# A three-block network in one kernel: block 1 normed ahead of its modulation, low halves on DVE, an unrolled conv FFN, and the bias store in sixteen transfers

## What is computed

```python
# block 1: both inputs are normed, scaled and shifted; then one dense product, retention and conv, 16 experts
sh1, sc1, g1, sh2, sc2, g2 = _modulation(c, w_ada, b_ada)          # silu(c) @ w_ada + b_ada
hc = _rms_norm(ctx, pre_mix_g) * (1.0 + csc1) + csh1               # context tokens
hx = _rms_norm(x,   pre_mix_g) * (1.0 + sc1)  + sh1                # the tokens themselves
... = split(hc @ w_in);  ... = split(hx @ w_in)
x = x + g1 * _rms_norm(mix_x, post_mix_g)
x = x + g2 * _rms_norm(_expert_choice_ffn(hx2, ...), post_ffn_g)
# block 2, second half
x = x + rmsnorm(merged @ w_out, mix_post_norm)
h = rmsnorm(x, ffn_pre_norm)
up = causal_dwconv(h @ w_ffn_up, ffn_conv_w, ffn_conv_b)           # 6144 channels, 3 taps
f_gate, f_val = split(up, 2)
x = x + rmsnorm((gelu(f_gate) * f_val) @ w_ffn_down, ffn_post_norm)
# block 3, attention with a relative bias: bias = rel_bias[t5_bucket(dist)], dist = query - key
```

## Time and profile before

| | |
|---|---|
| median of 3 runs | 2014.65 us (2014.63 to 2015.08) |
| the profiled execution's own time | 2014.23 us |
| its span, first to last instruction | 2012.4 us |
| mean granted clock of TensorE | 0.879 of full |
| PE / DVE / ACT / POOL busy | 1537.4 / 715.4 / 593.5 / 96.3 us |

### The profile page before, as it was taken

The page is one execution under the profiler, slowest core; times in us unless marked ns, Lnnn a source line. Parts: engine busy times, 40 slices in busy tenths (PEclk is TensorE's granted clock), DMA queues, the critical chain, the costliest instruction groups (busy, mean ns, idle before and its releaser), DMA issues.

```text
span 2012.4 us, 25017 instructions
## 1 busy us (share of the span) xinstructions
PE 1537.4 (76%) x10341; PEld 1036.4 (51%) x10341; DVE 715.4 (36%) x1136; ACT 593.5 (29%) x1009; POOL 96.3 (5%) x44
## 2 busy tenths in 40 slices
PE   4999886565666666566556569999879999898897
PEld 2787731111111111111111139989869888797897
DVE  3347320000000000000000028767667885558564
ACT  4443420000000000000000025765644553455453
POOL 1264300000000000000000000000000000000000
PEclk8999887888887878877788889999989998899899
DMA  9366559999999999999999983344554443443230
GB/s 402 135 251 243 240 242 427 429 429 428 429 429 428 429 428 429 429 429 428 428 429 428 429 350 143 134 147 148 161 150 164 174 155 138 157 150 133 85 126 22
DMA packets 48439, 570.10 MB, mean 283 GB/s; under 512 B 4592, under 2 KB 10736, under 8 KB 11888
## 3 DMA queue, kind: packets, MB, share of 16 engines
q1 hardware_dynamic: 40992, 556.81, 67.4%
q10 hardware_dynamic: 7376, 12.29, 2.5%
HBM read 564.89 MB, written 4.19 MB: 283 GB/s over the span
## 4 chain that ended last, share of the span: by engine, by line
PE 44%; DMA 39%; DVE 11%; ACT 3%; issue 2%; DVEq 1%; ACTq 1%; POOL 0%; SPq 0%
PE bank L1488 44%; DMA ring<-in_w_down 13%; DMA ring<-in_w_gate 12%; DMA ring<-in_w_up 12%; DVE ring_rounded L2078 2%; ACT work L1796 1%; DVE work L899 1%; DMA ring<-in_w_ada 1%; DVE rstd L2024 1%; ACT weights_high_rounded L1796 1%; DVE h_normed L2028 1%; DVE work L2028 1%; ACTq L660 1%; DVE work L895 0%; POOL ring_rounded L1473 0%
## 5 line engine op out<-in xcount | busy, mean ns | idle before, releaser
L1488 PE MATMUL bank<-ring,work 128*32 128x512 f32 x3008 | 481.2, 772 | 315.2 <-DMA ring<-in_w_up 126.4
L1796 ACT ACTIVATE work<-bank 128x256 f32<-128x256 f32 (+4 forms) x291 | 128.9, 453 | 1136.2 <-PE bank L1488 812.0
L1488 PEld LDWEIGHTS bank<-ring,work 128*32 128x32 f32 x3008 | 92.8, 125 | 671.3 <-DMA ring<-in_w_up 208.1
L2078 DVE TENSOR_TENSOR ring_rounded<-ring,weights_high_rounded 128x1024 fp32r<-128x1024 f32 x208 | 250.3, 1221 | 117.5 <-ACT weights_high_rounded L1796 117.4
L1796 ACT ACTIVATE weights_high_rounded<-ring 128x1024 fp32r<-128x1024 f32 x244 | 255.7, 1052 | 22.0 <-PE bank L1488 21.9
L2248 DVE TENSOR_TENSOR work<-work,bank 128x512 f32<-128x512 f32 x16 | 16.5, 1030 | 594.4 <-PE bank L1488 594.4
L1488 PE MATMUL bank<-h_high_rounded,weights_high_rounded 128*128 128x256 f32 x1296 | 202.1, 296 | 19.0 <-ACT h_high_rounded L1796 17.7
L1488 PEld LDWEIGHTS bank<-h_high_rounded,weights_high_rounded 128*128 128x128 f32 x1296 | 172.7, 194 | 36.6 <-issue 23.6
L1488 PE MATMUL bank<-h_high_rounded,ring_rounded 128*128 128x256 f32 x1296 | 181.1, 283 | 12.5 <-DVE ring_rounded L2078 12.0
L1488 PE MATMUL bank<-h_normed_rounded,weights_high_rounded 128*128 128x256 f32 x1296 | 181.3, 284 | 0.0
L1488 PEld LDWEIGHTS bank<-h_high_rounded,ring_rounded 128*128 128x128 f32 x1296 | 164.5, 193 | 15.7 <-DVE ring_rounded L2078 14.4
(11 more groups left out here) (225 smaller groups left out, 1168.2 us busy)
## 6 DMA issues: line engine op xcount, KB each, us to landing
ring<-in_w_down SPq DMA_DIRECT2D x64, 2048.0 KB, 16.3
ring<-in_w_gate SPq DMA_DIRECT2D x63, 2048.0 KB, 16.4
ring<-in_w_up SPq DMA_DIRECT2D x61, 2048.0 KB, 16.3
ring<-in_dense SPq DMA_DIRECT2D x60, 2048.0 KB, 8.0
ring<-in_w_ada SPq DMA_DIRECT2D x12, 2048.0 KB, 12.7
work<-in_w_up SPq DMA_DIRECT2D x3, 1024.0 KB, 13.3
bias_diagonals<-work ACTq DMA_DIRECT2D x2, 1532.0 KB
ring<-in_dense SPq DMA_DIRECT2D x2, 1024.0 KB, 18.8
```

The source lines that it names most:

```text
L1488: return nc.tensor.matmul(o, lhsT, rhs, start=start, stop=stop)
L1796: return nc.scalar.activation(o, i, f, **kw)
L2078: v.tensor_tensor(as_r(w), w, w_high[:, buffer, :], ALU.subtract).then_inc(s.w_low, 1)
```

## The change

Six edits, all in one diff.

1. **Start of block 1.** The sums of squares come ahead of ada products 1 to 3 on PE. DVE norms ctx and x (`CTXN`, `XN`) ahead of the modulation; when this is there, ACT (scale and bias) and DVE (`shifted_split`) each work out scaled and shifted tiles. The 655 KB of early constants are no longer part of the first constants' load but come after the second root. `first_jobs` takes the first four jobs tile by tile.
2. **Block 1's weight lows** (36) move from POOL to DVE, as `lows1` between its other operations. A 128x1024 reciprocal is two of 128x512 with a low between.
3. **Experts.** The last one is written out and ends the accumulation itself; the eight closing matmuls are gone.
4. **Bias store.** ACT's two DMAs become sixteen, one for each head and kind, each from one partition. SP issues them, behind rounds 1 to 5 of `dense2` (blocks 0 to 19) and ahead of block 20.
5. **FFN.** Unrolled. ACT applies one tap and the bias as it takes a unit out of PSUM; DVE adds the two shifted taps straight from PSUM; PE may reuse a bank when `conv_step` says that they are done. Gelu, product and splits of a pair follow at once.
6. **The wait for the store**, ahead of DVE's FFN before, is ACT's at unit 40 of 48.

```diff
 # SP
-            with sp.Fori(0, D2_BLOCKS // RING) as r:
+            def dense2_round(r):
                 for b in range(RING):
                     sp.wait_ge(s.ring_used, r * RING + (D2_BLOCK0 + b - RING + 1))
...
+            rounds_before = (L_SSM + 4) // (RING * UNITS) + 1
+            with sp.Fori(0, rounds_before) as r:
+                dense2_round(r)
+            sp.wait_ge(s.toep_sb, 3)
+            for kind in range(2):
+                for h in range(AH):
+                    sp.dma_start(d["toep"][kind * AH + h:kind * AH + h + 1],
+                                 spread(TW[h:h + 1, kind, :], 1, P)).then_inc(s.toep_stored, 16)
+            with sp.Fori(rounds_before, D2_BLOCKS // RING) as r:
+                dense2_round(r)
 # ACT, SSM units
                 if n == 3:
+                    fn(TW[0:AH, :, TOEP:TPITCH], ones[0:AH, 0:2].unsqueeze(2), ACT.Copy).then_inc(s.toep_sb, 1)
...
-                    act.wait_ge(s.toep_sb, 2)
-                    for kind in range(2):
-                        act.dma_start(d["toep"][kind * AH:(kind + 1) * AH, :, 0:TOEP],
-                                      spread(TW[0:AH, kind, 0:TOEP], 1, P)).then_inc(s.toep_stored, 16)
 # PE, FFN up
-            tensor_loop2(pe, dense_unit, L_UP, 3, normed, IN_AT["up"][0])
+            for u in range(2 * FT):
+                if u >= 4:
+
+                    pe.wait_ge(s.conv_step, taps_through(u - 4))
+                unit2(L_UP + u, normed, None if u else "up")
+            pe.wait_ge(s.conv_step, taps_through(2 * FT - 1))
 # ACT, FFN up
+            for u in range(2 * FT):
+                unit_done(d2_block(L_UP + u), block_ends(L_UP + u))
+                if u == 40:
+
+                    act.wait_ge(s.toep_stored, 32 * AH)
+                fn(ffn_conved(u), B[(PU2 + L_UP + u) % 4][:, 0:SEQ], ACT.Identity, scale=ffn_weight(u, 2),
+                   bias=par("ffn_conv_b", u, u + 1)).then_inc(s.dense_sb, 1)
+                weight_high(D1_UNITS + L_UP + u + AHEAD2)
 # DVE, FFN up (the loops with conv_pair go)
+            for k in range(FT):
+                for u in (2 * k, 2 * k + 1):
+                    tap(u, 1)
+                    weight_low(L_UP + u + AHEAD2)
+                    tap(u, 2)
+                    if u % 2 == 0 and k:
+                        split_low(FV[:, k - 1, :], UP[:, 2 * (k - 1), :])
+                dve.wait_ge(s.ffn_gelu, k + 1)
+                dve.wait_ge(s.conv_step, taps_through(2 * k + 1))
+                v.tensor_tensor(FV[:, k, :], FV[:, k, :], UP[:, 2 * k, :], ALU.mult).then_inc(s.act_full, 1)
 # experts, PE
-            for q in range(4):
-                last = mm(B[4 + q][:], ZERO[0:1, 0:P], ZERO[0:1, :], False, True)
-            last.then_inc(s.acc_done, 1)
+            expert(EXPERTS - 1, final=True)
 # block 1, DVE
-            norm_invert(0)
-            norm_invert(1)
+            for i, dst, src in ((0, CTXN, CTXR), (1, XN, X)):
+                norm_invert(i)
+                for half in (slice(0, 4), slice(4, KT)):
+                    v.tensor_tensor(dst[:, half, :], src[:, half, :], spread(RS[:, i, :], 1, 4),
+                                    ALU.mult).then_inc(s.first_normed, 1)
+            lows1(0, 1)
             modulation(0)
...
-            norm_shifted(0, HC, CTXR, A1[:, 1, :], MOD[:, 0:8, 1], CTXR)
-            norm_shifted(1, H, X, A1[:, 0, :], MOD[:, 0:8, 0], HH)
+            shifted_split(1, HC, CTXN, CTXR)
+            lows1(1, UNITS)
+            shifted_split(0, H, XN, HH)
```

More of the change, by code:

```diff
@@ L371, in tensor_dense2 @@
                        last).then_inc(s.ring_used if block_ends(unit) else s.dense_mm, 1)
[L373 to L381, removed]
         def conv_unit(u):
@@ L387, in conv_unit, with taps_through, ffn_weight, ffn_conved @@
             return dst, par(name + "_w", 4 * n, 4 * n + 4), par(name + "_b", n, n + 1)
+        def taps_through(u):
+            return 2 * u + 2
+        def ffn_weight(u, tap):
+            return par("ffn_conv_w", 3 * u + tap, 3 * u + tap + 1)
+        def ffn_conved(u):
+            return tiles(u - 1, 1) if u % 2 else tiles(48 + u // 2, 1)
         def tensor_block2(pe, mm, dense_unit, column_sum, column_sums):
@@ L504, in tensor_block2, with scalar_block2 @@
             column_sum(8, KT - 1)
[L506 to L527, removed]
+        def scalar_block2(act, fn, link, square, squares_of_x, root_table, root, unit_done, weight_high, split_high):
             def copy2(unit, dst, tile=None):
@@ L675, in scalar_block2 @@
                 split_high(HH[:, k, :], H[:, k, :])
[L677 to L693, removed]
+            for u in range(2 * FT):
[5 more added lines that the diff above has]
+                weight_high(D1_UNITS + L_UP + u + AHEAD2)
+                k = u // 2
+                if u % 2:
+                    act.wait_ge(s.conv_step, taps_through(u - 1))
                     fn(FV[:, k, :], FV[:, k, :], ACT.Gelu_apprx_tanh).then_inc(s.ffn_gelu, 1)
-                if k >= 18:
-                    split_high(UP[:, 2 * (k - 2), :], FV[:, k - 2, :])
+                elif k:
+                    split_high(UP[:, 2 * (k - 1), :], FV[:, k - 1, :])
+            split_high(UP[:, 2 * (FT - 1), :], FV[:, FT - 1, :])
             for n in range(KT):
@@ L1470, in _ @@
         def _(pool):
-            def low(block_no, sub, buffer):
-                w = unit_weights(block_no, sub)
-                nc.gpsimd.tensor_tensor(as_r(w), w, w_high[:, buffer, :], ALU.subtract).then_inc(s.w_low, 1)
-            for unit in range(D1_UNITS):
-                pool.wait_ge(s.w_high, unit + 1)
-                low(d1_block(unit), unit % UNITS, unit % HIGHS)
             for n in range(4):
@@ L1491, in arrived, with dense_unit @@
                 pe.wait_ge(ring_loaded[block_no % RING], uses(block_no))
-            def dense_unit(block_no, sub, bank, high, low, counts, base=None, first=True, last=True, turn=None):
+            def dense_unit(block_no, sub, bank, high, low, counts, base=None, first=True, last=True):
                 buffer = w_high[:, (counts - 1) % HIGHS, :]
-                if turn is not None:
-                    counts = turn + counts
                 parts = [("hh", buffer, high), ("lh", None, high), ("hl", buffer, low)]
@@ L1533, in column_sum @@
                 pe.wait_ge(s.norm_squared, KT * i + k + 1)
-                if i and k == 0:
+                if i > 1 and k == 0:
                     pe.wait_ge(s.norm_root, i)
-                last = mm(B[bank][:, 0:SEQ], ones[:], SQ[:, k, :], k == 0, k == KT - 1)
+                last = mm(B[bank][:, 0:SEQ], ones[:], (HH_plain if i == 1 else SQ)[:, k, :], k == 0, k == KT - 1)
                 if k == KT - 1:
@@ L1739, in expert @@
                                           k == 0, k == KT - 1)
-                        if not (isinstance(e, int) and 4 * half + b in EXTRA):
+                        if not (first and 4 * half + b in EXTRA):
                             last.then_inc(s.ring_used, 1)
@@ L2082, in weights_low, with lows1 @@
                     weight_low(unit)
+            def lows1(first, end):
+                for unit in range(first, end):
+                    dve.wait_ge(s.w_high, unit + 1)
+                    w = unit_weights(d1_block(unit), unit % UNITS)
+                    v.tensor_tensor(as_r(w), w, w_high[:, unit % HIGHS, :], ALU.subtract).then_inc(s.w_low, 1)
             def modulation(r):
@@ L2110, in _ @@
             last.then_inc(s.ramp_ready, 1)
-            dve.wait_ge(s.consts_in, 16)
+            lows1(4, 8)
+            dve.wait_ge(s.start_in, 32)
             dve.wait_ge(s.dense_sb, 2)
```

220 lines of the change are left out of this document (115 added, 105 removed).

## The result

The changed kernel takes 2043.2 us (median of 4 runs, 2039.67 to 2043.93) against 2014.87 (2014.63 to 2017.04) for the kernel before: 1.0135 times the time, 95% interval 1.0117 to 1.0152, 28.3 us slower. Its profiled execution took 2042.85 us (span 2041.1), 28.6 more than that of before.

What follows compares the result with a forecast made beforehand. PE bounds it wherever fed, DMA the experts. From 2014.2 us, block 1 -9.5, experts' end -3.6, FFN -20.4 and store +68.6 sum to +35.1: 2049.3 us; forecast's own range 2033 to 2066, 8 in 10 1969 to 2062.

Steps and rivals of the forecast that it cites:

- block 1's start and mix: Block 1: start gains 10.2 us, fewer POOL waits 0.7, two lows standing behind other work cost 1.4; net -9.5.
- experts' end: End of the experts: eight matmuls between the last product and ACT go away, -3.6 us.
- first up matmul, in times of before: FFN start: a 114 us store ahead of block 20 on SP's queue delays it to 1574.2 from 1505.62, +68.6 us.
- FFN: FFN's up product: PE stays the bound at conv-stage pace, one wait of about 4 us is left, -20.4 us.
- the overlap between groups: Store: reading ahead where one group of four partitions ends saves at most 24 us of 126; the middle, 12, was taken.
- The reading that decided: Old store: neither engines nor HBM limit it, but reading few partitions, about 25 GB/s per group of four.
- landing + 1.05 + 9.6: Ahead of the FFN: the first up matmul comes no sooner than block 20's landing plus these microseconds.
- The 9.3 us of ACT's hold: Bias store: freeing ACT of its 10.81 us issue would gain 9.3 us, but the slow store on SP swallows it.
- the account of DVE's room: FFN: a pair costs DVE 5.2 us against PE's 5.55, leaving 0.35 us to spare.
- rival (c): FFN: with a fast store DVE becomes the bound, giving back 13 us, and 4 in block 1; 1988 us, chance 0.05.
- Rival (a): Store: engines limit, so sixteen make it fast, 28 us, and all gains stand, -42.8; 1971 us, chance 0.22.
- Rival (b): Store: both groups of four partitions are read at once, 63 us at 50 GB/s; 1998 us, chance 0.12.

Runs made afterwards that it cites:

- e9: The kernel before with the three edits of block 1 alone (start, lows on DVE, last expert): 1997.44 us against 2012.67, ratio 0.9918.
- e4: The kernel before with the store edit alone (sixteen transfers on SP): 2078.31 us, 62.8 above before, ratio 1.031.
- e5: The kernel before with the FFN edit alone, ACT waiting for the old store at unit 40: 1994.26 us, 20.9 below before, ratio 0.989.
- e1: The changed kernel with the store's heads in the order 0,4,1,5,2,6,3,7 instead of 0 to 7: 2000.22 us, ratio 0.9925 to before.
- e2: The changed kernel with the store as two transfers of eight partitions each, at the same place in SP's queue: 1997.23 us, ratio 0.9908 to before.
- e3: The changed kernel with the bias table made in all 128 partitions and stored by two transfers on SP's queue: 1969.33 us, ratio 0.9766 to before.
- e6: The kernel before with the table made in all 128 partitions, its two store transfers still on ACT's queue: 2006.56 us, 8.6 below before, ratio 0.9951.
- e8: e3 with the third tap of the FFN's conv back on DVE, from PSUM, ACT only copying: 1974.13 us, 4.8 above e3.
- e7: e3 with block 1's 36 weight lows given back to POOL: 1975.15 us, 5.8 above e3.

## Why the prediction was right

The point was 2049.3, the result 2043.2 (profiled 2042.85): slower, as forecast, by the mechanism forecast, and inside the forecast's own range (2033 to 2066). By its terms, in the traces of before and after:

| term | forecast | measured | from |
|---|---|---|---|
| block 1's start and mix | -9.5 | -8.9 | squares after the experts 12.6 sooner, less 3.6 |
| experts' end | -3.6 | -3.6 | the closing matmuls' 3.64 are gone |
| first up matmul, in times of before | +68.6 | +62.3 | 1555.29 + 12.6 - 1505.62 |
| FFN | -20.4 | -20.8 | start of block 3's long run +28.84, less 49.67 |
| sum | +35.1 | +28.8 | 28.84 before rounding |

The measured column is one pair of traces, and each entry is good to about 2 us: by the means of ten traces (under e9) the first line is -10.7. Its entries add up by the way they are taken, so the sum is no test of its own; the test is that e4, e5 and e9 measure the parts one by one (+62.8, -20.9, -15.2).

**The store is the term that was mis-sized**, by 6.3 us, and that it is no more is in part luck: three errors in its working partly cancel. The rate of one group of four partitions is 27.4 GB/s (7.18 us a transfer), not 25, so 115 us of reading instead of 126. The store's packets pass from 1433.5 to about 1535.3, where GB/s rises from 25 or so to over 300 in the DMA view: 102 us, so the overlap between groups was 13 us, near the 12 taken. That is 12 us less than the 114 forecast, at the low end of its 102 to 126. But the store began 1.5 us later than forecast, and block 20 then took 9.5 us to land, not 4.9. SP had put three loads of the ring into the queue by 1537.6, and 3.69 MB passed in those 9.5 us, of which block 20 is 2.1: it had to share the engines, and the forecast took it to be alone:

```profile
1525.57 12.05 SPq L1408 DMA_DIRECT2D ring<-in_dense  x3
```

A packet took 0.69 us, not the 0.9 that was named as a sign; still three times the 0.22 of before.

The Trainium skill ("SBUF — State Buffer", "Door 1: The DMA port swizzle") gives 27.6 GB/s for partitions 0 to 3; the trace agrees, with 27.4. Its figure was nearer to the measured rate than the 25 that the sum used.

**The reading that decided**, from the last microsecond of the old store (fewer engines, shorter packets, nearly the same rate), is borne out by e1 (order alone, 43 us), e2 and e3. That all sixteen engines shared one transfer, as the change made them, was true and no help.

**The stage behind it**, landing + 1.05 + 9.6, held: 1544.84 to 1555.29 is 10.45. The 9.3 us of ACT's hold were swallowed in the change, as forecast, and show as 8.6 in e6, where nothing else holds the stage's end.

**FFN**: PE stays the bound, one wait of 3.25 where about 4 was said. But the account of DVE's room was too tight. It added the mean durations of DVE's operations. In e8 the six groups' busy times add up to 87.1 us in a window of 80 us: operations in a row overlap at their ends, so a sum of durations overstates what they take. In the change DVE is busy 17.23 of 20 us, which leaves about 0.8 us a pair in place of the 0.35 that was worked out, so rival (c) was less likely than the 0.05 it had.

**Block 1**: the fifth job came at 59.80, forecast 60.3. The terms for the waits in the middle (+0.7, -1.4) and for the end of the mix (nothing) are known only in their sum with the start.

Rival (a), 1971, is what e3 makes of the same edits with a fast store: 1969.3. Rival (b), 1998, is what e1 and e2 make with both groups read at once: 2000.2 and 1997.2. Their prices were right; their condition wasn't met.

## What to carry to other kernels

Count the partitions that are read at a time, not the engines that a transfer spreads over: here one partition after another out of a group of four gave 27 GB/s, both groups together about 50, all 128 partitions about 370. Nothing between 8 and 128 was tried. A table that is to be written many times is better made in all partitions first (here one small copy and a wider stationary operand). A queue that carries weights takes only stores that are fast. When an edit bundle gets slower, don't give up the bundle: here one part cost 63 us and hid 36 us of gains.

## What was not expected

- A DMA issue can last as long as a transfer that is under way, since it waits for room in the queue: the same two stores of 1024 rows take 10.81 us of ACT from eight partitions, 1.83 from 128; sixteen of 128 rows take 5.8 us each on average on SP (93.2 / 16) when one group of partitions is read after the other, 3.5 (56.08 / 16) when the two alternate.
- A DVE that is busy 19.34 of 20 us held PE up only at the end (e8), since operations in a row overlap (87.1 us of them in 80).
- Executions of one kernel spread by up to 5.4 us on one chip (e3: 1966.49 to 1971.81; the kernel before beside e5 to e8: 2013.91 to 2019.35), more than the 0.45 of the first three runs of before; on the chip of e9 the median of before was 2.5 us lower than beside e5. In e3's profiled execution PE did 674 matmuls from 1520 to 1600, in e7's 689, both at a granted clock of 1.00; the cause of these 2% stays open. Differences under 3 us are read from traces, not from medians, and by the spread under e9 a pair of traces is good to about 2 us.
